# A two-layer attention, delta-rule and expert trunk on one core: four modulation slabs of the first layer loaded by the Activation queue and multiplied between convolution columns

## The chip, the core and the metric

The kernel runs on one core of a Trainium2 chip. The core has TensorE (PE, matmuls and transposes), VectorE (DVE), ScalarE (ACT, also called Activation), GpSimd (POOL) and SyncE (SP, which only issues transfers here). Sixteen DMA engines move data between HBM and the on-chip memory. ACT and POOL can issue transfers too, each on a queue of its own. The metric is the device time of one execution in microseconds, given as the median of several runs.

## The reference, cut to what matters

Two layers work on 128 context tokens and 256 latent tokens of width 1024, in float32.

```python
def modulation(cvec, lw):
    m = jax.nn.silu(cvec) @ lw["ada_w"] + lw["ada_b"]          # ada_w: (1024, 6144)
    return jnp.split(m[..., None, :], 6, axis=-1)               # sh1, sc1, g1, sh2, sc2, g2

def latent_layer(x, c, k_ctx, v_ctx, s_ctx, lw):                # context_layer: the same with c_ctx
    sh1, sc1, g1, sh2, sc2, g2 = modulation(c, lw)
    h = modulate(rms_norm(x, lw["norm1_g"]), sh1, sc1)
    zq, zk, zv, zqkv, zg, zb, za = jnp.split(h @ lw["w_in"], SPLITS, axis=-1)
    q, k, v = na_heads(zq, zk, zv, lw)
    o_na = neighbourhood_attention(q, k, v, k_ctx, v_ctx, lw["na_rpb"])
    gq, gk, gv, gg, gbeta = gdn_inputs(zqkv, zb, za, lw, axial=True)   # conv of 5 taps, SiLU, L2 norm
    o_g, _ = gdn_bidirectional(gq, gk, gv, gg, gbeta, s_ctx)           # chunked delta rule
    o_mix = jnp.concatenate([o_na, gdn_output(o_g, zg, lw["gdn_norm_g"])], axis=-1)
    x = x + g1 * (o_mix @ lw["w_out"])
    return x + g2 * hier_moe(modulate(rms_norm(x, lw["norm2_g"]), sh2, sc2), lw)
```

For the first half of a layer only `sh1` and `sc1` of the modulation are needed. `g1` is wanted at the output projection, and the last three at the expert part.

## The kernel before, in words

**Slabs.** Weights come in slabs of 2 MB. A layer's `ada_w` is twelve slabs: slab `i` holds 256 of the 1024 rows and 2048 of the 6144 columns, so four slabs (`SHARE`) make one third of the modulation. `w_in` is seven slabs (`win`) and `w_out` two (`wout`). They are held in a ring of five slots. SP loads them in the order of `PRE[l]` (`pre_slabs`), each after the job that last read its slot (`slab_done`). For the first layer the list is ada 0 to 3, the seven win slabs in the order 6, 3, 4, 5, 0, 1, 2, then ada 4 to 11 of this layer and ada 0 to 3 of the next, and wout. The second layer has no next one and so eight ada slabs behind its win slabs. The win slabs lie in slots 4, 0, 1, 4, 3, 4, 3; slot 2 holds none. All slabs behind them alternate between slots 4 and 3 (`LATE_SLOTS`).

**What else the ring holds.** From the convolution on, slots 0, 1 and 2 are the work space of the delta rule: `inv` and `inv_t[0]` lie in slot 0, `gT` and `inv_t[1]` in slot 1, `decays`, `sub_v` and `half_y` in slot 2. `decays` is first written by ACT at convolution column 5.

**One slab's product.** `ada_product` on PE multiplies 16 times into bank 3, which no other job uses in these stages. After four slabs DVE copies the bank to `mrow` (`ada_row`), PE turns it into columns (`ada_cols`, 8 small matmuls into a bank that DVE empties), and DVE adds the bias (`ada_col`).

**Order of a layer.** (1) Norm and modulation of the three token tiles, with the gate projection (win 6) between them. (2) The convolution stage: twelve column groups `f` of w_in (win 3, 4, 5), each 16 matmuls of 128x384; behind each, transposes of an earlier group (`conv_cols`), sums of decays (`decay_sums`, f = 5 to 10), and at f = 4 `gate_sums`, which waits for the small weights (`weights_in`). ACT empties each group to `conv_in`, DVE convolves, ACT applies SiLU, PE transposes back, ACT empties again. (3) Heads: `head_cols`, `head_products` for three token tiles, whose banks DVE turns into `weighed` and `inv`; then token-major projections (win 0, 1, 2), while DVE solves small triangular blocks (`substitution`). SP and POOL move these blocks through HBM (`blocks_out`, `blocks_back`, `inv_t`). (4) The mixing stage: ten steps of attention (`scores`, `probs_cols`, `weigh`), with the delta rule's parts `rule(k)` and the ada products between them, at 22 numbered points. `mixing_plan` spreads the products: with twelve slabs, the first before the steps and the others at points 4, 5, 6, 8, 9, 11, 12, 14, 15, 16 and 18; with eight, the others at 5, 7, 9, 11, 13, 15 and 17. (5) `gate_rows(1)`, transposes of `g1`, then the output projection, router and token lists. (6) Experts, whose weights (1 MB pieces) SP loads into the ring and the arena as pieces are given back.

**Banks.** DVE's jobs rotate over three PSUM banks and ACT's over three others: PE may fill one when the job three before it has been emptied (`dve_bank`, `act_bank`).

The work around the change is in the order written out by hand in each engine's block; waits are semaphore counts.

Of the kernel before, what the change touches and what calls it, by code (L numbers as in the profile page):

```python
# [14 lines left out]
P = 128  # L15
# [6 lines left out]
DEPTH = 2  # L22
# [10 lines left out]
SLAB = 4096  # L33
N_ADA, N_WIN, N_OUT = 12, 7, 2
EARLY = 4
PRE_SLOTS = 5
WIN_ORDER = [6, 3, 4, 5, 0, 1, 2]
WIN_SLOTS = [4, 0, 1, 4, 3, 4, 3]
# [20 lines left out]
N_STEPS = len(STEPS)  # L59
POINTS = 2 * N_STEPS + 2  # L60
RULE_AT = 3
SHARE = 4
BLOCK = 32
BLOCKS = P // BLOCK
MATS = TILES * GH
# [46 lines left out]
def pre_slabs():  # L112

    out = []
    for l in range(DEPTH):
        ada = [("ada", l, i) for i in range(EARLY, N_ADA)]
        if l + 1 < DEPTH:
            ada += [("ada", l + 1, i) for i in range(EARLY)]  # L120
        first = [("ada", 0, i) for i in range(EARLY)] if l == 0 else []
        out.append(first + [("win", l, j) for j in WIN_ORDER] + ada + [("wout", l, j) for j in range(N_OUT)])
    return out


def mixing_plan(slabs):
# [135 lines left out]
def program(nc, x_prompt, x_sample, c, cache_k, cache_v, state_ssm, c_ctx, ada_w, ada_b, norm1_g,  # L262
# [10 lines left out]
    with ctx:  # L273
# [236 lines left out]
        def place_of(slabs, i):  # L510

            first_win = [name[0] for name in slabs].index("win")
            if i < first_win:
                return i
            i -= first_win
            return WIN_SLOTS[i] if i < N_WIN else LATE_SLOTS[(i - N_WIN) % 2]
# [3 lines left out]
            earlier = [name for name in slabs[:i] if pre_slot[name] == pre_slot[slabs[i]]]  # L520
            return earlier[-1] if earlier else None

        for slabs in PRE:
            for i, name in enumerate(slabs):
                pre_slot[name] = place_of(slabs, i)
                held[pre_slot[name]] += 1
                pre_turn[name] = held[pre_slot[name]]

        def arrived(eng, *name):
            eng.wait_ge(slab_in[pre_slot[name]], 16 * pre_turn[name])  # L530
# [23 lines left out]
        def _(pe):  # L554
# [72 lines left out]
                ada_product(("ada", 0, i))  # L627
            ada_cols(("ada", 0, EARLY - 1), b_mods)
            for l in range(DEPTH):
                mixing = [name for name in PRE[l][EARLY if l == 0 else 0:] if name[0] == "ada"]  # L630
                plan = mixing_plan(mixing)

                def point(p):
# [74 lines left out]
                def ba_sums():  # L708

                    pe.wait_ge(dve_emptied, job["ba_part", l])  # L710
                    b = dve_bank("ba", l)
                    for t in range(TILES):
                        last = mm(b[:, t * BA:(t + 1) * BA], ba_part[:, t * P:(t + 1) * P], tab("pick_ba"))
                    last.then_inc(for_dve, 1)
# [31 lines left out]
                for f in range(12):  # L746
                    slab = ("win", l, 3 + f // 4)
                    if f % 4 == 0:
                        arrived(pe, *slab)
                    if f == 4:  # L750
                        gate_sums()
                    w = wide(pre_slot[slab])
                    b = act_bank("conv", l, f)
                    for k in range(KC):
                        last = mm(b[:, 0:TOK], w[:, k, (f % 4) * P:(f % 4 + 1) * P], hT[:, k, :], k == 0, k == KC - 1)
                    last.then_inc(for_act, 1)
                    slab_job[slab] = ("act", jobs["act"])
                    if f == 0:
                        ba_sums()
                    if 5 <= f < 11:  # L760
                        decay_sums(f - 5)
                    if f >= 2:
                        conv_cols(f - 2)
# [10 lines left out]
                def head_products(t):  # L774

                    pe.wait_ge(act_emptied, job["gT", l, t, 0])
                    for pair in range(2):
# [3 lines left out]
                            last = mm(b[:, 256 * i:256 * i + 256], gT[:, t, h, 0, :], flat(gT[:, t, h]))  # L781
                        last.then_inc(for_dve, 1)

                arrived(pe, "win", l, 0)
                head_cols(0)
                token_major(0, 0)
# [2 lines left out]
                head_cols(2)  # L789
                head_products(1)  # L790
                head_products(2)
                token_major(0, 1)
                token_major(0, 2)
                conv_cols(10)
# [484 lines left out]
        def _(sp):  # L1279
# [51 lines left out]
            for l in range(DEPTH):  # L1331
# [39 lines left out]
                        src = src[:, :, j * 512:(j + 1) * 512]  # L1371
                    sp.dma_start(dst, src).then_inc(slab_in[pre_slot[name]] if done is None else done, 16)

                first_mixing = [i for i, name in enumerate(PRE[l]) if name[0] == "ada" and i >= N_WIN][0]
                for i, name in enumerate(PRE[l]):
                    if i == first_mixing + 1:
                        blocks_back()
# [105 lines left out]
        def _(act):  # L1483
# [51 lines left out]
            for l in range(DEPTH):  # L1535
# [17 lines left out]
                modulated(l, 1, 2)  # L1553
                gate_tile(1)
                gate_tile(2)

                def token_tile(which, t):
                    b = filled("win", l, which, t)
# [43 lines left out]
                for c in range(12):  # L1602
# [2 lines left out]
                        act.wait_ge(conv_ready, 12 * l + c - 1)  # L1605
                    f(conv_in[:, c % 2, 2:2 + CTX], b[:, 0:CTX])
                    f(conv_in[:, c % 2, CTX + 6:CTX + 6 + LAT], b[:, CTX:TOK]).then_inc(act_emptied, 1)
                    if 5 <= c < 11:
                        decay_exp(c - 5)
                    if c >= 2:  # L1610
# [14 lines left out]
                def head_cols(t):  # L1625
                    for s in (1, 0):
                        b = filled("gT", l, t, s)
                        f(gT[:, t, :, 1 - s, :], b[:].rearrange("p (h n) -> p h n", h=GH)).then_inc(act_emptied, 1)

                head_cols(0)  # L1630
                act.wait_ge(act_emptied, job["conv_back", l, 9])
                token_tile(0, 0)
# [172 lines left out]
        def _(dve):  # L1805
# [119 lines left out]
            ada_col(("ada", 0, EARLY - 1))  # L1925
            for l in range(DEPTH):
                mod = mods[:, l]
                plan = mixing_plan([name for name in PRE[l][EARLY if l == 0 else 0:] if name[0] == "ada"])

                def point(p):  # L1930

# [184 lines left out]
                dve.wait_ge(gexp_ready, l + 1)  # L2116
                if l == 0:
                    dve.wait_ge(weights_in, 16 * N_SMALL)
                head_products(0)
                head_products(1)  # L2120
                vec.memset(sub_v[32:64], 0.0)
                head_products(2)
                convolve(10)
                convolve(11)
                qk_sums(0, 0)
# [443 lines left out]
        def _(pool):  # L2569
# [7 lines left out]
            for l in range(DEPTH):  # L2577
# [17 lines left out]
                mask_bias(0)  # L2595

                pool.wait_ge(for_act, job["conv", l, 7])
                for d in range(2):
                    gp.memset(inv_t[d], 0.0).then_inc(zeroed, 1)
                pool.wait_ge(raw_ready, 3 * (l + 1))  # L2600
# [132 lines left out]
```

## Time and profile before

| what | value |
|---|---|
| median of 3 runs | 1226.54 us (1225.91 to 1232.42) |
| profiled execution, its own time | 1225.16 us |
| its span in the profile | 1223.1 us |
| PE busy | 1104.9 us, 90% of the span |
| DVE, ACT, POOL busy | 555.9, 291.9, 110.1 us |
| DMA | 333.30 MB, mean 273 GB/s |
| mean granted clock of PE | 0.961 |

The profile is one execution. Its times are counted from the start of the span. "Idle before, releaser" names what ended an engine's idle time. A granted clock of 1.00 is 2.4 GHz, and 0.50 is 1.2 GHz. PEq, SPq and ACTq are sequencers: issues of transfers stand there. L577 is the helper for all matmuls and L580 that for all transposes, so tiles and shapes tell the jobs apart: an ada product is `bank<-ring,silu_w` x16, convolution columns are `bank<-hT,ring` 128x384 x16, `ada_cols` is `bank<-const,mrow` x8, the gate rows are `bank<-const,mod`.

### The profile page before, as it was taken

Reading aid. Unit: us, or ns where it says so; the run is one execution under the profiler, and the core shown is the slowest. Engines: PE = TensorE matmul, PEld = TensorE weight load, DVE = VectorE, ACT = ScalarE, POOL = GpSimd, SP = SyncE. Lnnn points to the kernel's source line nnn. Section 1 sums busy time; section 2 is a strip of 40 time slices with the busy share of each in tenths; the row PEclk is TensorE's granted clock in tenths of the full one; section 3 lists DMA queues with packets and bytes.
Section 4 is the critical chain, followed back from the end, with each engine's and each line's share of the span. In section 5 each row is a group of like instructions: output and inputs, shape, how many; then the busy total and the mean of one; then the engine's idle time right before and its main releaser. Section 6 shows DMA issues by size and latency. Waiting matters only on the chain.

```text
span 1223.1 us, 18762 instructions
## 1 busy us (share of the span) xinstructions
PE 1104.9 (90%) x7521; PEld 548.7 (45%) x7521; DVE 555.9 (45%) x1416; ACT 291.9 (24%) x717; POOL 110.1 (9%) x126
## 2 busy tenths in 40 slices
PE   4899999898999999978789999989999999997776
PEld 1455544475556333322245655446745733332222
DVE  1257896466447311210162678945744742111124
ACT  0347512323122110000021672232331310100000
POOL 0020023310001000000011000242000100000001
PEclk9899999799997999999989999988999799999998
DMA  8670134967935999999983203376495399999996
GB/s 356 204 196 1 70 95 130 288 259 282 407 155 215 416 424 425 424 426 424 421 335 109 72 1 95 138 164 235 183 379 200 145 418 421 425 424 425 425 424 264
DMA packets 90794, 333.30 MB, mean 273 GB/s; under 512 B 29631, under 2 KB 32071, under 8 KB 59975
## 3 DMA queue, kind: packets, MB, share of 16 engines
q1 hardware_dynamic: 80999, 299.66, 62.7%
q0 software_dynamic: 7392, 23.93, 5.8%
q10 hardware_dynamic: 2304, 8.39, 1.7%
q8 instruction: 63, 1.03, 0.3%
q14 instruction: 36, 0.29, 0.1%
HBM read 314.38 MB, written 17.56 MB: 271 GB/s over the span
## 4 chain that ended last, share of the span: by engine, by line
PE 71%; SPq 11%; DMA 9%; DVE 5%; issue 2%; ACT 2%; DVEq 0%; ACTq 0%
PE bank L577 66%; SPq L1318 10%; PE bank L580 5%; DMA arena<-in_moe_w_dram 4%; DMA ring<-in_ada_w_dram 3%; DMA ring<-in_w_in_dram 2%; ACT arena L1497 2%; DVE x L1831 1%; DVE ring L1831 1%; DVE x L1823 1%; DVE arena L1823 1%; DVE small L2144 0%; DVE small L1831 0%; DVE bank L1823 0%; SPq L1407 0%
## 5 line engine op out<-in xcount | busy, mean ns | idle before, releaser
L577 PE MATMUL bank<-ring,arena 128*32 128x512 f32 (+1 forms) x2272 | 328.6, 583 | 26.4 <-issue 12.5
L577 PE MATMUL bank<-arena 128*32 128x512 f32 (+3 forms) x1600 | 267.3, 562 | 18.7 <-DMA arena<-in_moe_w_dram 10.3
L1497 ACT ACTIVATE arena<-bank 128x512 f32<-128x512 f32 (+3 forms) x292 | 124.3, 467 | 577.0 <-PE bank L580 392.5
L577 PE MATMUL bank<-ring,hT 128*128 128x512 f32 x576 | 256.9, 600 | 3.7 <-DMA ring<-in_w_in_dram 2.7
L577 PEld LDWEIGHTS bank<-ring,arena 128*32 128x32 f32 (+1 forms) x2272 | 99.0, 114 | 214.4 <-issue 212.0
L577 PEld LDWEIGHTS bank<-ring,hT 128*128 128x128 f32 x576 | 108.5, 193 | 129.5 <-issue 126.3
L577 PE MATMUL bank<-hT,ring 128*128 128x384 f32 x384 | 128.3, 488 | 0.1
L1823 DVE TENSOR_TENSOR arena<-bank,mrow 128x512 f32<-128x512 f32 x36 | 24.9, 692 | 225.2 <-PE bank L577 225.2
L577 PEld LDWEIGHTS bank<-arena 128*32 128x32 f32 (+2 forms) x1600 | 80.6, 122 | 95.1 <-issue 78.3
L577 PEld LDWEIGHTS bank<-hT,ring 128*128 128x128 f32 x384 | 71.2, 190 | 46.9 <-issue 1.3
L580 PE MATMUL bank<-const,arena 128*128 128x128 f32 x443 | 66.7, 287 | 18.2 <-DMA x<-in_x_prompt_dram 8.5
L580 PEld LDWEIGHTS bank<-const,arena 128*128 128x128 f32 x443 | 52.2, 145 | 63.1 <-issue 57.1
L1823 DVE TENSOR_TENSOR hT<-hT,bank 128x512 f32<-128x512 f32 x18 | 19.3, 1074 | 133.0 <-PE bank L577 133.0
L1831 DVE SCALAR_TENSOR_TENSOR arena<-arena,cols 128x388 f32<-128x388 f32 x96 | 62.5, 651 | 3.4
L577 PE MATMUL bank<-ring 32*32 32x32 f32 (+3 forms) x976 | 58.6, 248 | 4.1 <-DVE ring L1831 2.3
L577 PE MATMUL bank<-ring,silu_w 128*32 128x512 f32 x384 | 48.6, 627 | 10.9 <-DMA ring<-in_ada_w_dram 10.9
L577 PEld LDWEIGHTS bank<-ring 32*32 32x32 f32 (+2 forms) x976 | 51.4, 156 | 14.8 <-issue 9.8
L1823 DVE TENSOR_TENSOR ring<-ring 112x30 f32<-112x30 f32 (+14 forms) x120 | 50.4, 420 | 4.1
L1497 ACT ACT_TABLE_LOAD x38 | 48.8, 1283 | 13.2 <-DVE cols L1836 10.0
L1497 ACT ACTIVATE hT<-bank 128x512 f32<-128x512 f32 (+1 forms) x32 | 18.9, 591 | 131.7 <-PE bank L577 94.6
L1497 ACT ACTIVATE arena<-bank,small 128x128 f32<-128x128 f32 (+2 forms) x74 | 34.9, 508 | 36.4 <-DVE small L2144 33.8
L2668 POOL DMA_INDIRECT arena<-tok_dram,idx x16 | 15.4, 962 | 242.5 <-issue 106.8
(162 smaller groups left out, 866.4 us busy)
## 6 DMA issues: line engine op xcount, KB each, us to landing
ring<-in_moe_w_dram SPq DMA_DIRECT2D x120, 1024.0 KB, 18.8
arena<-in_moe_w_dram SPq DMA_DIRECT2D x72, 1024.0 KB, 18.1
ring<-in_ada_w_dram SPq DMA_DIRECT2D x24, 2048.0 KB, 8.6
ring<-in_w_in_dram SPq DMA_DIRECT2D x14, 2048.0 KB, 9.7
ring<-in_w_out_dram SPq DMA_DIRECT2D x4, 2048.0 KB, 8.9
expert_dram<-arena ACTq DMA_DIRECT2D x16, 512.0 KB, 8.3
tok_dram<-arena POOLq DMA_DIRECT2D x6, 512.0 KB, 2.9
arena<-in_na_rpb_dram SPq DMA_DIRECT2D x16, 96.0 KB, 7.2
```

Of the source, the lines that this page charges most:

```text
L577: return nc.tensor.matmul(out, lhsT, rhs, start=start, stop=stop)
L580: return nc.tensor.transpose(out, src, ident[0:rows_, 0:rows_])
L1318: sp.dma_start(dst.rearrange("p (o k n) -> p o k n", o=1, k=src.shape[2]), src).then_inc(done, 16)
L1497: return nc.scalar.activation(out, in_, func, **kw)
L1823: return vec.tensor_tensor(out, a, b, op)
L1831: return vec.scalar_tensor_tensor(out, a, s, b, op0, op1)
L2668: pool.indirect_dma_start(out=x_e[:, c_ % 2, :], out_offset=None, in_=tok_dram, in_offset=bass.IndirectOffsetOnAxis(ap=idx[:, column(c_):c ...
```

## The change

In the first layer ada slabs 4 to 7 leave SP's list. ACT issues their loads, into slots 2, 0, 0 and 1 (`MIDDLE_SLOTS`): the first after the third gate tile, the second when convolution group 4 has been emptied (slot 0's win slab was last read by group 3), the third and fourth at group 8. PE multiplies the first two behind groups 2 and 6, the other two behind the loop over the groups, and makes the columns after the head products. ACT waits for the first product before it writes `decays`, and for the fourth before it writes `gT`; POOL waits for the fourth before it clears `inv_t`; DVE copies the row ahead of its head products. The mixing stage of the first layer is left with eight slabs and `mixing_plan` places them. The second layer is as before.

```diff
+MIDDLE_LAYERS = 1
+MIDDLE_SLOTS = [2, 0, 0, 1]
...
+def middle_slabs(l):
+    return [("ada", l, EARLY + i) for i in range(SHARE)] if l < MIDDLE_LAYERS else []
+
+def mixing_slabs(l):
+    here = [("ada", l, i) for i in range(EARLY, N_ADA)] + [("ada", l + 1, i) for i in range(EARLY) if l + 1 < DEPTH]
+    return [name for name in here if name not in middle_slabs(l)]
...
 # tensor
-                mixing = [name for name in PRE[l][EARLY if l == 0 else 0:] if name[0] == "ada"]
+                mixing, middle = mixing_slabs(l), middle_slabs(l)
...
                     if f == 0:
                         ba_sums()
+                    if middle and f in (2, 6):
+                        ada_product(middle[f // 4])
                     if 5 <= f < 11:
                         decay_sums(f - 5)
...
+                for slab in middle[2:]:
+                    ada_product(slab)
                 arrived(pe, "win", l, 0)
                 head_cols(0)
...
                 head_products(1)
                 head_products(2)
+                if middle:
+                    ada_cols(middle[-1])
                 token_major(0, 1)
...
 # scalar
                 gate_tile(2)
+                middle = middle_slabs(l)
+                def load_middle(i):
+                    src = ada_w[l].rearrange("(k p) n -> p k n", p=P)[:, 2 * i:2 * i + 2, 2048:4096]
+                    s = pre_slot[middle[i]]
+                    act.dma_start(slot(s).rearrange("p (k n) -> p k n", k=2), src).then_inc(slab_in[s], 16)
+                if middle:
+                    if l == 0:
+                        act.wait_ge(ada_full, EARLY)
...
+                    load_middle(0)
...
+                    if middle and c == 4:
+                        act.wait_ge(for_act, job["conv", l, 3])
+                        load_middle(1)
+                    if middle and c == 8:
+                        act.wait_ge(ada_full, slab_job[middle[1]][1])
+                        load_middle(2)
+                        act.wait_ge(for_act, job["conv", l, 7])
+                        load_middle(3)
+                    if middle and c == 5:
+                        act.wait_ge(ada_full, slab_job[middle[0]][1])
                     if 5 <= c < 11:
                         decay_exp(c - 5)
...
+                if middle:
+                    act.wait_ge(ada_full, slab_job[middle[3]][1])
                 head_cols(0)
...
 # vector
+                if middle:
+                    ada_row(middle[-1])
                 head_products(0)
                 head_products(1)
                 vec.memset(sub_v[32:64], 0.0)
                 head_products(2)
+                if middle:
+                    ada_col(middle[-1])
                 convolve(10)
...
 # gpsimd
                 pool.wait_ge(for_act, job["conv", l, 7])
+                if middle_slabs(l):
+                    pool.wait_ge(ada_full, slab_job[middle_slabs(l)[3]][1])
                 for d in range(2):
                     gp.memset(inv_t[d], 0.0).then_inc(zeroed, 1)
```

## Rows read from the trace of the kernel before

**Rows 1.** Page, 40 slices of the span, what the DMA engines moved.
```profile
GB/s 356 204 196 1 70 95 130 288 259 282 407 155 215 416 424 425 424 426 424 421 335 109 72 1 95 138 164 235 183 379 200 145 418 421 425 424 425 425 424 264
```

**Rows 2.** Chain that ended last, 60 to 360 us, by line.
```profile
by line: PE bank L577 80.0%; DMA ring<-in_ada_w_dram 10.7%; PE bank L580 4.0%; ACT arena L1497 1.9%; DVE ring L1831 1.1%; SPq L1359 0.9%; issue 0.7%; DVE arena L1823 0.6%; SPq L1372 0.1%; ACT hT L1497 0.1%; ACTq L1488 0.0%; DVEq L2079 0.0%;
```

**Rows 3.** Windows: busy us of PE, PEld, DVE, ACT, POOL; clock; DMA share; GB/s.
```profile
60.00:80.00 20.00, 20.00 (x77) 11.03 (x76) 7.06 (x15) 6.11 (x11) 0.00 (x0) 1.00 0.65 164
...
100.00:120.00 20.00, 19.97 (x67) 11.53 (x66) 11.97 (x21) 16.90 (x44) 1.41 (x2) 1.00 0.00 1
...
214.00:222.00 8.00, 4.77 (x41) 2.48 (x40) 2.32 (x5) 2.77 (x12) 6.85 (x10) 0.91 0.93 187
222.00:232.00 10.00, 8.73 (x199) 5.42 (x200) 4.28 (x11) 3.58 (x9) 1.18 (x1) 0.50 1.08 265
...
841.00:851.00 10.00, 9.47 (x122) 6.68 (x119) 7.66 (x19) 2.95 (x9) 0.00 (x0) 1.00 0.73 281
```

**Rows 4.** Waits of PE, 200 to 312 us: total, times, longest.
```profile
PE bank L577 <- DMA ring<-in_ada_w_dram: 7.0, 3, 3.0
```

**Rows 5.** Timeline of PE, layer 0, mixing stage and after: start, duration.
```profile
214.26 1.92 PE L577 MATMUL bank<-ring,silu_w 128*32 128x512 f32 x16
...
252.04 0.96 PE L577 MATMUL bank<-const,mrow 128*128 128x8 f32 x8
252.92 1.93 PE L577 MATMUL bank<-ring,silu_w 128*32 128x512 f32 x16
254.78 0.88 PE L577 MATMUL bank<-arena 128*64 128x128 f32 x12
...
310.93 1.97 PE L580 MATMUL bank<-const,mod 128*128 128x128 f32 x16
...
386.70 0.37 PE L577 MATMUL bank<-tokid_b,arena 128*128 128x2 bf16 x9
```

**Rows 6.** The same of layer 1.
```profile
811.08 1.92 PE L577 MATMUL bank<-ring,silu_w 128*32 128x512 f32 x16
...
833.99 2.80 PE L577 MATMUL bank<-ring,silu_w 128*32 128x512 f32 x16
...
898.20 1.99 PE L580 MATMUL bank<-const,mod 128*128 128x128 f32 x16 [0.28 <-DVE mod L1823]
...
973.99 0.37 PE L577 MATMUL bank<-tokid_b,arena 128*128 128x2 bf16 x9
```

**Rows 7.** Timeline of PE and DVE, convolution stage and heads of layer 0.
```profile
69.53 10.57 PE L577 MATMUL bank<-hT,ring 128*128 128x384 f32 x32
...
85.76 0.96 PE L577 MATMUL bank<-small,const 128*128 128x12 f32 x8
...
104.08 1.02 PE L577 MATMUL bank<-arena,const 128*128 128x512 f32 x2
...
152.36 1.12 DVE L1831 SCALAR_TENSOR_TENSOR ring<-bank,small,ring 128x128 f32<-128x128 f32 x4
152.80 13.90 PE L577 MATMUL bank<-ring,hT 128*128 128x512 f32 x32
```

**Rows 8.** Timeline of ACT, POOL and ACT's queue: start, duration.
```profile
62.38 0.60 ACT L1497 ACTIVATE arena<-bank 128x512 f32<-128x512 f32 x1 [6.27 <-PE bank L577]
...
82.63 4.66 POOL L2574 TENSOR_TENSOR arena<-arena,gdn_g 128x512 f32<-128x512 f32 x3 [74.75 <-DMA w_rt<-in_moe_w_re_dram]
...
92.44 0.72 ACT L1497 ACTIVATE arena<-bank 128x128 f32<-128x128 f32 x3 [4.17 <-PE bank L577]
...
441.53 0.36 ACTq L1776 DMA_DIRECT2D expert_dram<-arena  x1
```

**Rows 9.** Page, DMA issues: count, KB each, median us to landing.
```profile
ring<-in_ada_w_dram SPq DMA_DIRECT2D x24, 2048.0 KB, 8.6
...
expert_dram<-arena ACTq DMA_DIRECT2D x16, 512.0 KB, 8.3
...
x<-in_x_sample_dram SPq DMA_DIRECT2D x1, 1024.0 KB, 24.3
```

More of the change, by code:

```diff
@@ L35 @@
 EARLY = 4
+SHARE = 4
+MIDDLE_LAYERS = 1
+MIDDLE_SLOTS = [2, 0, 0, 1]
 PRE_SLOTS = 5
@@ L61 @@
 RULE_AT = 3
-SHARE = 4
 BLOCK = 32
@@ L117, in pre_slabs @@
     for l in range(DEPTH):
-        ada = [("ada", l, i) for i in range(EARLY, N_ADA)]
-        if l + 1 < DEPTH:
-            ada += [("ada", l + 1, i) for i in range(EARLY)]
         first = [("ada", 0, i) for i in range(EARLY)] if l == 0 else []
-        out.append(first + [("win", l, j) for j in WIN_ORDER] + ada + [("wout", l, j) for j in range(N_OUT)])
+        out.append(first + [("win", l, j) for j in WIN_ORDER] + mixing_slabs(l) + [("wout", l, j) for j in range(N_OUT)])
     return out
+def middle_slabs(l):
[3 more added lines that the diff above has]
+    return [name for name in here if name not in middle_slabs(l)]
 def mixing_plan(slabs):
@@ L521, in held_before @@
             return earlier[-1] if earlier else None
[L523 to L527, printed above, removed]
+        for l, slabs in enumerate(PRE):
+            fore = slabs.index(("win", l, WIN_ORDER[-1])) + 1
+            places = [(name, place_of(slabs, i)) for i, name in enumerate(slabs)]
+            for name, s in places[:fore] + list(zip(middle_slabs(l), MIDDLE_SLOTS)) + places[fore:]:
+                pre_slot[name] = s
+                held[s] += 1
+                pre_turn[name] = held[s]
         def arrived(eng, *name):
@@ L1372, in load_slab @@
                     sp.dma_start(dst, src).then_inc(slab_in[pre_slot[name]] if done is None else done, 16)
-                first_mixing = [i for i, name in enumerate(PRE[l]) if name[0] == "ada" and i >= N_WIN][0]
+                first_mixing = PRE[l].index(mixing_slabs(l)[0])
                 for i, name in enumerate(PRE[l]):
@@ L1555, in _ @@
                 gate_tile(2)
+                middle = middle_slabs(l)
[6 more added lines that the diff above has]
+                        act.wait_ge(ada_full, EARLY)
+                    else:
+                        act.wait_ge(es["y_full"], 3 * BATCHES * l)
+                    load_middle(0)
                 def token_tile(which, t):
@@ L1927, in _ @@
                 mod = mods[:, l]
-                plan = mixing_plan([name for name in PRE[l][EARLY if l == 0 else 0:] if name[0] == "ada"])
+                middle = middle_slabs(l)
+                plan = mixing_plan(mixing_slabs(l))
                 def point(p):
```

## The prediction

> **What bounds the kernel now.** I read the page's slices first; at full load the DMA engines move 424 to 425 GB/s, and there are two stretches where they move almost nothing, the convolution stages of the two layers [rows 1]. Then the chain of waits, cut to 60 to 360 us, the region that the diff touches: 80% of it is TensorE (PE) itself, and 10.7% is `ring<-in_ada_w_dram`, the loads of modulation slabs [rows 2]. The windows say where the room is: from 100 to 120 us PE is busy 19.97 of 20 us at a granted clock of 1.00, and the DMA share is 0.00; ScalarE (ACT) is busy 16.9 there [rows 3]. Then PE's own waits in the mixing stage: 7.0 us in three waits for such slabs [rows 4]. So layer 0's mixing stage, which I measure from its first product (214.26) to the gate rows (310.93), is 96.67 us long [rows 5] and passes twelve slabs through two ring slots. Layer 1's mixing stage has only eight slabs and is otherwise the same code: from 811.08 to 898.20, 87.12 us [rows 6]. The new plan of layer 0 has eight slabs too, at the points that the same formula gives, so layer 1 is the nearest row for it.
>
> What follows the gate rows takes the same time in both layers: to the first list of tokens it is 75.77 us in layer 0 and 75.79 in layer 1 (386.70 and 973.99 [rows 5, 6]). So a shift of layer 0's gate rows should reach the end of the span whole.
>
> **The change, part by part.**
>
> *Products moved forward.* A slab's product is 16 matmuls; at full clock the next instruction starts 1.86 us after it (252.92 to 254.78 [rows 5]). In the convolution stage PE has no hole to put it in [rows 3], so four of them cost 4 x 1.86 = 7.44 us there.
>
> *Their columns.* `ada_cols` costs 0.88 us (252.04 to 252.92 [rows 5]). It takes a bank from the rotation of three that VectorE (DVE) empties, right after `head_products(2)`, and so must wait until DVE is through with the job three before, the second pair of tile 1. DVE ends that at 152.36 + 1.12 = 153.48, while PE is free at 152.80 now and goes on with token columns that need an ACT bank [rows 7]. That is a new wait of 0.68 us. It stays when all is later, because DVE's work on the pairs starts with PE's first pair. DVE's own additions are a row copy, ahead of the first pair, for which DVE waits for PE anyway, and a column add of 0.2 us on a chain that moves later by less than PE does. Sum of the front: 7.44 + 0.88 + 0.68 = 9.0 us.
>
> *The loads and the waits that they bring.* An issue on ACT's queue costs ACT 0.36 us [rows 8]; four make 1.4 us, in a stage where ACT has 3.1 of 20 us free [rows 3], and each product gives it 1.86 us more. I take nothing. The first slab is issued once ACT has emptied the third gate tile, 62.38 + 0.60 = 62.98 [rows 8], and is wanted when convolution columns 2 are done, 69.53 + 10.57 = 80.1 [rows 7]: 17.1 us later. Ada loads landed after 8.6 us in the median [rows 9]. But this one shares the engines with a projection slab and the bias rows: a share of 0.65 from 60 to 80 us, 13.0 us of full work [rows 3]; 2.1 MB at 424 GB/s [rows 1] add 5.0, and 62.7 + 18.0 = 80.7 is the latest by plain addition. Early bound 71.6 and no wait, late bound a wait of 0.6 us; I take 0, since the late bound needs this slab to be served last of all. What SP has queued there counts too: its small weights let GpSimd (POOL) start at 82.63 [rows 8], and PE asks for them in `gate_sums` at 85.76 [rows 7]. Pushed back by the whole 5.0 us they come at 87.6, and PE then asks at 85.76 + 1.86 = 87.6: no cost, and no margin. The Trainium skill (DMA: Bandwidth & Descriptors, section "Issuing engines are not separate DMA queues") says that transfers of SP, ACT and POOL run on the same 16 engines and interleave, and that another issuer saves only issue time. By that rule a second queue wins no bandwidth: the 5.0 us come on top, as I have added them, and the sum stays. Stores of 512 KB on ACT's queue, the size of a quarter slab, landed after 8.3 us beside SP's expert loads [rows 9], which agrees.
>
> The second slab is issued after columns 4 are emptied, 92.44 + 0.55 now [rows 8] and 94.85 then, and wanted at the end of columns 6, 104.08 + 1.86 = 105.9 [rows 7]: 11.1 us against 8.6. The third and fourth go out two columns of 6.35 us and two products after that, near 121.5, and are wanted from 140; 8.6 + 5.0 us fit into that, with idle engines [rows 3]. ACT's new waits are for products that PE did before the bank which ACT has just emptied; behind them stand decay exponentials, squares and the banks that PE asks for next, none late unless a slab is. POOL's clearing of `inv_t` now waits for the fourth product, near 144; its results are wanted after 200 us. SP's own order only gets shorter. All of this at 0.
>
> *What the mixing stage gives back.* Taken out are four products, one column step and the slab waits: 7.44 + 0.88 + 7.0 = 15.3 us if nothing takes their place. But the products also filled PE's waits in the softmax chain (scores, DVE's maxima, ACT's exponentials, transposes). So the bounds are -15.3, by removal, and -9.55, by layer 1 (87.12 against 96.67). I take -9.55: it is the same eight-slab code, measured.
>
> *Sum.* 9.0 - 9.55 = -0.55 us. The profiled execution took 1225.16 us, 2.06 more than its span and 1.38 less than the median of the three runs. So 1224.6 for such an execution, and 1226.0 beside the median of 1226.54. A change under 0.5% (6.1 us) can hardly be told from none for this kernel.
>
> **Rivals.**
>
> *The removal counts in full.* If no wait takes the place of the old ones, the sum is 9.0 - 15.3 = -6.3 and the time 1220.2 us. For it: layer 0 has DMA waits in its mixing stage and layer 1 the same chain without them, so the two need not be alike in the rest. Against it: 15.3 minus 9.55, 5.8 us, is what layer 1 shows as not given back, and I know of nothing in its code that layer 0 lacks.
>
> *The first slab comes late* (the case on the other side). Its product stands in PE's order behind columns 2, so from 17.1 us after its issue each microsecond late is one of the total. A load behind a full queue took 24.3 us here (`x<-in_x_sample_dram` [rows 9]); that would be 7.2 us of wait, 1233.2 us, slower. For it: two queues at full load beside each other have not been seen in this stage. Against: the engines have 7 us of room in these 20, and the 24.3 us were behind 8 MB.
>
> *The clock falls more often.* PE was busy 4.77 of 8 us, and then the granted clock is 0.50, its level of 1.2 GHz, from 222 to 232 us [rows 3]. In layer 1 a product as late as 833.99 still takes 2.80 us in place of 1.93 [rows 5, 6]. With fewer fillers, light steps could fall to that level again; one stretch of 10 us costs about 5, so 1231. Layer 1 is back at 1.00 in the window from 841 on [rows 3] with the same plan, which speaks against it. The Trainium skill (TensorE: Matmul & The Clock Gate, section "HAM oscillation — how this bites in real kernels") says that waits between bursts of matmuls let the clock go back to half; the trace agrees at these two places.
>
> *It does not remove the slab waits.* Two slots remain, and each slab still waits for the product before the last. Then 9.0 - 8.3 = +0.7, 1227.2. Layer 1 shows that eight slabs in two slots pass in 87 us, so this is unlikely.
>
> **How the numbers follow.** Forecast, with leftovers from -4 to +3 us around 1226.0: 0.74. Removal in full, 1220.2: 0.08. First slab late, 1233: 0.08. Clock, 1231: 0.06. Slab waits stay, 1227: 0.04. The full removal straddles the bound of 6.1 us and the late slab lies just above it: faster 0.06, same 0.85, slower 0.09. The range reaches down to near the full removal, 1221.0, and up to 1230.5, past half of the late-slab wait.
>
> **What would show it.** Right: four products of 1.9 us more between 80 and 150 us, the head products 7.4 us later, a wait of some 0.7 us ahead of new `mrow` columns there, the first mixing product at 223.3 and the gate rows at 310.4, with 87 us between them and no PE wait for `in_ada_w_dram`; all later stages moved by the same half microsecond. Wrong: a PE wait for a slab at columns 2 or 6, a wait in `gate_sums`, a granted clock under 1.00 before 200 us, or a mixing stage under 84 or over 90 us. What would upset the number most is a layer 0 that is not like layer 1.

## The result: 0.6% faster, and outside the range

The changed kernel takes 1220.34 us in the median of 20 runs (1213.79 to 1226.76), the kernel before beside it 1226.64 us (20 runs, 1218.43 to 1233.84). The ratio is 0.9941, 95% interval 0.9923 to 0.9959: 7.2 us less, 5.0 to 9.4. The forecast was 1226.0 and the range ended at 1221.0. The profiled execution of the changed kernel is one of its long ones, 1226.13 us, with a span of 1223.9 us at a mean granted clock of 0.962. So its length as a whole says nothing, and its stages have to be read one by one: over the whole span PE's gaps by "issue" (idle time that ends with no semaphore) add up to 34.0 us in it and to 26.9 us in a second profile of the same kernel, 25.1 and 33.7 us in two profiles of the kernel before.

"The front" is from here on all that stands ahead of the first product of the mixing stage. Changed kernel, waits of PE for DVE from 60 to 210 us (in total, times, longest; 0.4 us for ACT stand beside them, as in the kernel before):

```profile
PE bank L589 <- DVE ring L1875: 1.6, 3, 0.7
```

What the DMA engines moved in the 40 slices, and the issues of modulation slabs on ACT's queue (count, KB each, median us to landing; SP's twenty had 8.7 us):

```profile
GB/s 357 203 234 103 202 95 99 216 225 242 378 104 318 420 424 424 424 426 424 418 211 136 46 39 97 114 193 202 199 400 147 215 415 425 424 425 424 425 422 195
...
ring<-in_ada_w_dram ACTq DMA_DIRECT2D x4, 2048.0 KB, 9.4
```

The empty fourth slice of the kernel before [rows 1] now carries 103 GB/s. Timeline of PE, front (start, duration):

```profile
80.02 1.92 PE L589 MATMUL bank<-ring,silu_w 128*32 128x512 f32 x16
...
106.16 1.92 PE L589 MATMUL bank<-ring,silu_w 128*32 128x512 f32 x16
...
140.28 3.64 PE L589 MATMUL bank<-ring,silu_w 128*32 128x512 f32 x32
...
160.82 1.03 PE L589 MATMUL bank<-const,mrow 128*128 128x8 f32 x8 [0.65 <-DVE ring L1875]
```

The four products stand at 80, 106 and 140 us, and the columns behind a wait of 0.65 us. Nothing waits for a slab. The two marks of the mixing stage of layer 0 answer to [rows 5]:

```profile
223.25 1.92 PE L589 MATMUL bank<-ring,silu_w 128*32 128x512 f32 x16
...
304.83 1.39 PE L592 MATMUL bank<-const,mod 128*128 128x128 f32 x11
```

The front is 223.25 - 214.26 = 8.99 us longer. The mixing stage is 304.83 - 223.25 = 81.58 us in place of 96.67. The stage behind the gate rows, up to the first list of tokens at 377.44, is 72.61 us in place of 75.77. Waits of PE in the mixing stage, the changed kernel and then the kernel before (there beside the 7.0 us for slabs [rows 4]):

```profile
PE bank L589 <- ACT arena L1515: 4.1, 10, 0.7
PE bank L592 <- DVE arena L1867: 2.3, 1, 2.3
PE bank L592 <- DVE arena L1871: 2.1, 2, 1.2
PE bank L589 <- DVE ring L1875: 0.3, 1, 0.3
```

```profile
PE bank L580 <- DVE arena L1823: 2.9, 1, 2.9
PE bank L577 <- ACT arena L1497: 2.9, 7, 0.5
PE bank L580 <- DVE arena L1827: 1.0, 1, 1.0
```

The slab waits are gone. The waits for ACT and DVE grow from 6.8 to 8.8 us. Removal in full, less these 2.0 us, is 15.3 - 2.0 = 13.3 us.

Windows over whole stages: the kernel before (mixing stage of layer 0, of layer 1, stage behind the gate rows), then the changed one (the same three):

```profile
214.26:310.93 96.67, 82.58 (x957) 53.46 (x957) 52.79 (x138) 29.69 (x98) 13.04 (x15) 0.93 0.81 282
811.08:898.20 87.12, 76.37 (x885) 52.13 (x885) 51.95 (x137) 29.85 (x98) 13.33 (x15) 0.90 0.68 226
310.93:386.70 75.77, 72.84 (x325) 49.14 (x324) 40.31 (x151) 17.91 (x42) 1.62 (x3) 0.91 0.59 234
```

```profile
223.25:304.83 81.58, 72.82 (x885) 50.08 (x885) 51.00 (x136) 29.59 (x98) 11.54 (x12) 0.96 0.71 237
807.63:894.97 87.34, 76.86 (x885) 52.08 (x884) 51.86 (x137) 29.86 (x98) 13.17 (x15) 0.90 0.68 225
304.83:377.44 72.61, 68.85 (x324) 44.85 (x324) 40.24 (x151) 17.69 (x42) 1.62 (x3) 0.98 0.57 229
```

These six rows hold a part of the answer. In one execution of the changed kernel the two mixing stages, both with eight slabs and both with 885 matmuls, last 81.58 and 87.34 us. The column to look at is the granted clock: 0.96 against 0.90. A mean of 0.90 over 87.12 us is (1 - 0.90) x 2 x 87.12 = 17.4 us at 0.50 (17.1 by the records of the clock); 0.96 over 81.58 us is 6.5 (6.8). The stage that I used as the measure, layer 1 of the kernel before, was such a slow one, with a gap of 1.64 us by "issue" besides. Layer 0 of the kernel before, with which I compared it, had 13.7 us at 0.50 and no such gap. So the clock alone parts those two by little; what it is worth is worked out below.

### The profile page after: what moved, and what is told of

The parts are those of the page before. It is cut to its first block, busy times and chain, and to the rows that moved or that the text cites. A ratio compares the mean times of both kernels' runs of the same rounds, so it can differ in the third digit from the quotient of the medians.

```text
span 1223.9 us, 18765 instructions
## 1 busy us (share of the span) xinstructions
PE 1103.7 (90%) x7521; PEld 540.6 (44%) x7521; DVE 554.1 (45%) x1416; ACT 291.9 (24%) x717; POOL 109.7 (9%) x126
## 4 chain that ended last, share of the span: by engine, by line
PE 71%; SPq 10%; DMA 7%; DVE 6%; issue 4%; ACT 2%; ACTq 0%; DVEq 0%
PE bank L589 67%; SPq L1336 9%; PE bank L592 4%; DMA ring<-in_w_in_dram 2%; ACT arena L1515 2%; DMA ring<-in_moe_w_dram 2%; DMA arena<-in_moe_w_dram 2%; DVE small L2193 1%; DVE x L1875 1%; DVE ring L1875 1%; DVE arena L1867 1%; DVE x L1867 1%; DVE bank L1867 1%; DVE small L1875 0%; SPq L1425 0%
## 5 line engine op out<-in xcount | busy, mean ns | idle before, releaser
L589 PE MATMUL bank<-ring,arena 128*32 128x512 f32 (+1 forms) x2272 | 337.8, 594 | 33.6 <-issue 21.5
L589 PE MATMUL bank<-arena 128*32 128x512 f32 (+3 forms) x1600 | 272.6, 564 | 19.2 <-DMA arena<-in_moe_w_dram 9.8
L589 PEld LDWEIGHTS bank<-arena 128*32 128x32 f32 (+2 forms) x1600 | 81.1, 123 | 89.5 <-issue 72.4
L1875 DVE SCALAR_TENSOR_TENSOR arena<-arena,cols 128x388 f32<-128x388 f32 x96 | 65.1, 678 | 3.4
L589 PEld LDWEIGHTS bank<-ring 32*32 32x32 f32 (+2 forms) x976 | 51.1, 154 | 14.7 <-issue 8.5
L1515 ACT ACTIVATE arena<-x 128x512 f32<-128x512 f32 (+1 forms) x18 | 13.9, 771 | 96.9 <-DVE x L1867 68.9
## 6 DMA issues: line engine op xcount, KB each, us to landing
ring<-in_w_in_dram SPq DMA_DIRECT2D x14, 2048.0 KB, 10.2
```

Of the source, the lines that this page charges most:

```text
L589: return nc.tensor.matmul(out, lhsT, rhs, start=start, stop=stop)
L1515: return nc.scalar.activation(out, in_, func, **kw)
L1875: return vec.scalar_tensor_tensor(out, a, s, b, op0, op1)
```

## The experiments

All were timed in five rounds, beside the kernel before on the same chip. Ratios are to that kernel.

**The two kernels again.** No edit: the changed kernel, and the kernel before.

> The changed kernel once more, unchanged, for a second profile and more times. Theory A (removal in full): the first layer's mixing stage, first product to gate rows, is 81.6 us again within 1 us, whatever the clock does elsewhere, and the ratio is 0.993 to 0.996. Theory B (clock): the stage's length follows the time that TensorE spends at 0.50 in it: 78.2 us plus half of the low time, so 81.6 with 6.8 us low and about 85 with 13.7; the ratio then depends on how often each kernel meets the low clock.

> The kernel before against itself: how far two equal kernels part in this measurement, and a second profile. Both theories: ratio 1.000 within 0.002. Theory A: mixing stage of the first layer 96.7 within 1 us. Theory B: 89.8 us plus half of the low time in it, and a span that changes by some 0.4 us for each microsecond of low clock.

Measured: 1220.39 us, ratio 0.9950 (0.9929 to 0.9971), and 1224.15 us, 0.9996 (0.9976 to 1.0015). The gain repeats. The profiles give other stages, though: the mixing stage of layer 0 is 98.77 us in the kernel before and 81.48 in the changed one, and that of layer 1 is 85.77 and 85.57. The same code spreads by microseconds from one execution to the next. Neither theory holds for both kernels: theory A has its 81.6 us and misses the 96.7, theory B has 98.3 us for the kernel before (89.8 and half of 17.1), which fits, and 79.9 for the changed one (78.2 and half of 3.4), which does not.

**The modulation slabs 4 to 7 left out.** From the changed kernel, without their loads, products, row, column step and waits. In their place `mods` of the gate and the second shift are copied from the first shift.

```diff
-                    if middle and f in (2, 6):
-                        ada_product(middle[f // 4])
...
-                for slab in middle[2:]:
-                    ada_product(slab)
...
-                    ada_row(middle[-1])
+                    vec.tensor_copy(mods[:, 0, 16:24, :], mods[:, 0, 0:8, :])
+                    vec.tensor_copy(mods[:, 0, 24:32, :], mods[:, 0, 0:8, :])
```

> The changed kernel without its four middle slabs at all: no loads, products, row or columns for them; DVE copies the first layer's shift over the gate and second shift, so 8 MB are not read and the output is another. The mixing stage keeps its eight slabs. Tells the price of the front alone. If the front costs 9.0 us and reaches the end whole, this is 9.0 faster than the changed kernel, near 1211 beside 1226.6, a ratio of 0.987. Rival: the front is partly hidden by something that ends last anyway, then only 3 to 5 us under the changed kernel, 0.990 to 0.992. Mixing stage as in the changed kernel, 79 to 87 us by its clock.

Measured: 4291.71 us, ratio 3.50. With these values the path for crowded experts ran (the profile reads 937 MB from HBM in place of 314), so this time says nothing on the question. The next version takes the negative of the first shift as the second:

```diff
-                    vec.tensor_copy(mods[:, 0, 24:32, :], mods[:, 0, 0:8, :])
+                    ts(mods[:, 0, 24:32, :], mods[:, 0, 0:8, :], -1.0)
```

> As the run that left the four slabs out, but with a stand-in for their modulation that keeps the experts' token counts under their limits (gate from the first shift, second shift from its negative), so that the path for crowded experts is not taken. No loads, products, row or columns for the four slabs. Front price of 9.0 us whole: the first mixing product at 214.3 to 215, the mixing stage 81 to 87 us, and 9 us under the changed kernel, near 1211, ratio 0.987 to 0.988. Rival (front hidden in part): 0.990 to 0.992.

Measured: 1217.19 us, ratio 0.9923 (0.9899 to 0.9948). Its first mixing product starts at 214.12 us, so all of the front's 9 us is gone in the profile, but its mixing stage had 17.1 us of low clock and took 86.53. By time it is 0.22%, 2.7 us, under the changed kernel (0.9923 against 0.9945, the mean of the latter's two ratios), with intervals of 0.2 to 0.25% on each side. So the expected 9.0 us did not come by time. Its six runs spent 96 us at the lower clock in the mean (from each run's span and mean clock), and the kernel before beside them 84. At 0.30 us each (worked out below) that is 3.7 us, so the run is too blunt to price the front.

**Three loads left out of the kernel before.** The slabs that PE waited for; their products read what lies in the slots.

```diff
+        SKIPPED = [("ada", 0, 6), ("ada", 1, 2), ("ada", 1, 3)]
...
-                held[pre_slot[name]] += 1
+                held[pre_slot[name]] += 0 if name in SKIPPED else 1
...
+                    if name in SKIPPED:
+                        continue
```

> The kernel before without the loads of the three slabs for which TensorE waited in the first layer's mixing stage (its third, eleventh and twelfth); their products stay and read what lies in the slot, so the modulation is another. Tells the waits from the products. If the slab waits are the only thing that a load costs there, the mixing stage is 7.0 us shorter, 89.7, and the ratio 0.994 to 0.995. Rival: the softmax chain takes half of it back, 93 us and 0.997. A clock effect would show as a stage off by half of the difference in low time.

Measured: 1218.84 us, ratio 0.9948 (0.9928 to 0.9968), 6.4 us less. The mixing stage is 89.94 us, with 1.3 us of slab wait left and 6.8 us of low clock. The ratio is the one expected if a load costs its wait and nothing else. With the products kept, the slab waits alone are worth what they lasted (7.0 - 1.3 = 5.7 us, and 92.9 - 87.9 = 5.0 us once the lower clock and the gaps are taken off as in the table below). This already speaks against the prediction's term, which left 9.55 us for waits, four products and a column step together.

**The first mixing product behind the first `weigh`,** in both layers of the changed kernel.

```diff
-                ada_product(mixing[0])
...
                     weigh(step)
+                    if step == 0:
+                        ada_product(mixing[0])
```

> The changed kernel with the first product of the mixing stage behind the first weigh, in both layers, so that it fills TensorE's wait for DVE's scaled scores (2.3 us in the first layer, 3.0 in the second). If the chain of the softmax only needs to start earlier, probs_cols(0) and (1) come 1.86 us earlier in each layer: 3.7 us off, and more if the low clock starts later or not at all, up to 8. Rival: the next waits (1.2 us at probs_cols(2)) grow by what this one loses, and nothing changes.

Measured: 1218.74 us, ratio 0.9939 (0.9916 to 0.9961). The interval holds the changed kernel's ratio, so the gain of some 1 us is not shown. The wait in layer 0 fell from 2.26 to 1.32 us.

**The same change in both layers.**

```diff
-MIDDLE_LAYERS = 1
+MIDDLE_LAYERS = 2
```

> The changed kernel with the same four slabs moved in the second layer too (its mixing stage keeps four). There TensorE waits for no slab now, so nothing but the place of the products changes. If products only move: front +9.0, mixing -8.3, so +0.7 and more where the softmax chain takes its waits back; I expect +3, ratio to the kernel before 0.997. If moving them also shortens the stretch at low clock as it did in the first layer: -3, ratio 0.992.

Measured: 1221.71 us, ratio 0.9951 (0.9931 to 0.9971). Where no slab wait is to be removed, moving four products buys nothing: layer 1 from its first products with `x` (628.77 us, in the changed kernel 625.54) to the mixing stage takes 190.97 us in place of 182.09, so 8.9 more, and the mixing stage 77.93, or 72.4 with its 10.2 us of low clock and its gap of 2.4 taken off, so 7.6 less than 80.0. That is close to the bare move of the products (+0.7 us expected), and neither the +3 nor the -3 is shown.

**The keys scaled early:** POOL's `keys_at_end(0)` ahead of `bias_rows(pool, l, 1)`, both layers.

```diff
-                bias_rows(pool, l, 1)
                 keys_at_end(0)
+                bias_rows(pool, l, 1)
```

> The changed kernel with POOL's first scaling of keys ahead of its eight bias transfers in both layers, so that it no longer runs beside DVE's scaling of scores in the second layer (two passes of 256 columns there took 1.36 to 1.66 us in place of 0.76). If that overlap is what makes the second layer's wait 3.0 us instead of 2.25, the wait falls to 2.3 and the passes to 0.76; the first layer does not change. Time: 0.7 us off, or 2 to 4 if the stretch at low clock (10 to 14 us in the second layer, 3 to 7 in the first) hangs on the length of that wait.

Measured: 1222.27 us, ratio 0.9949 (0.9925 to 0.9974). The wait of 3.0 us in layer 1 fell to 2.3 and DVE's two passes ahead of it from 1.49 to 0.76, as expected, and that moved no time that can be seen. What its profile shows besides is the clearest case of the second disturbance beside the clock, the gaps by "issue". Timeline of PE, layer 0:

```profile
238.49 0.65 PE L589 MATMUL bank<-ring 32*32 32x32 f32 x53
243.76 0.84 PE L589 MATMUL bank<-ring 32*32 32x32 f32 x43 [4.62 <-issue]
```

and what the DMA queues did from 241 to 242.5 us (packets, MB, share of 16 engines):

```profile
q8 instruction: 1, 0.02, 4.3%
```

PE stops for 4.62 us in the midst of 96 equal matmuls, with no semaphore to wait for. From 234 to 241 us the instruction queue moved nothing; at 241.13 us one block of 16 KB starts on it, lands after 1.03 us, and 1.6 us later PE goes on. All 23 such gaps in the mixing stages of the thirteen profiles (all but that of the run with crowded experts) end the same way, 1.3 to 1.6 us after a block of this queue has landed. That the block held PE's instructions is inferred from this timing. The Trainium skill (Trainium Architecture — The Big Picture, section "Inside one NeuronCore") has each engine run a stream of instructions of its own. That this stream came late here, in mid-kernel, is what the timing suggests; no run changed it.

**Fillers.** Dummy matmuls of 128x512 while PE would wait for the softmax chain: eight per mixing stage in the kernel before, seven in the changed one. Their output is not read. Each of these calls stands as two matmuls in the trace.

```diff
+                def filler(n_):
+                    if jobs["dve"] >= 3:
+                        pe.wait_ge(dve_emptied, jobs["dve"] - 2)
+                    for _ in range(n_):
+                        mm(bank[jobs["dve"] % 3][:], ident, const[:, 0:512])
...
+                    filler({1: 5, 2: 2}.get(step, 0))
                     probs_cols(step)
```

> The kernel before with eight dummy matmuls of 128x512 added per mixing stage (six ahead of the probability transposes of step 1, two ahead of those of step 2), whose output nobody reads: they keep TensorE at work while it would wait for the softmax chain. Theory A (the eight slabs taken out are worth about 13.2 us of mixing stage at an undisturbed clock): with less low clock in the stage it is 92 to 94 us in layer 0 with its three slab waits left. Rival B (my prediction's proxy, 9.55): the stage stays near 96. In time about 1224 to 1226, or 2 to 4 below if the fillers spare low clock.

> The changed kernel with seven such dummy matmuls per mixing stage (five and two). Theory A: 79 to 81 us in layer 0 and the same in layer 1, so 13 us under the twelve-slab stage of the run beside it, and as a whole 4.2 us shorter than that run's kernel (9.0 paid in front, 13.2 given back). Rival B: 87 us in both layers, and the two kernels within 1 us of one another.

Measured: 1233.61 us, ratio 1.0046 (1.0022 to 1.0069), and 1224.92 us, 0.9985 (0.9958 to 1.0013). The mixing stages of layer 0 are 97.78 and 86.94 us, that of layer 1 in the second kernel is 88.60. These lengths miss theory A's (92 to 94 and 79 to 81) and look like rival B's (96 and 87), but they hold the fillers' own cost. The six ahead of step 1 in the kernel before:

```profile
219.26 5.42 PE L577 MATMUL bank<-const 128*128 128x512 f32 x12
```

That is 0.90 us for each filler, 5.42 + 1.98 = 7.4 us for the eight, and they took the place of 3.9 us of waits for DVE. So a stage gets 3.5 us longer, which is what its length says once the lower clock and the gaps are taken off (96.4 us against 92.9). The difference of the two kernels is 10.84 us in the profiles, with no microsecond at 0.50 in the longer stage and 6.8 of them in the shorter. At 0.30 us each (worked out below), and with "issue" gaps of 1.4 and 1.9 us taken off, it is 97.78 - 1.4 - (86.94 - 1.9 - 2.0) = 13.3, of which up to 0.9 is the one filler more. By the ratios it is 7.5 us net of the front (3 to 12 with both intervals), up to 1.8 of it the two fillers more, where theory A had 4.2 and rival B under 1. The fillers lean to theory A and do not decide by themselves.

They did spare low clock: the twelve runs of each kernel spent some 72 and 67 us at the lower clock in the mean, those of the kernel before beside them 90. But they cost more than that gives back.

**The front alone.** The changed kernel's work in the convolution stage, and all twelve slabs in the mixing stage as before.

```diff
-    return [("ada", l, EARLY + i) for i in range(SHARE)] if l < MIDDLE_LAYERS else []
+    return [("mid", l, EARLY + i) for i in range(SHARE)] if l < MIDDLE_LAYERS else []
...
-    return [name for name in here if name not in middle_slabs(l)]
+    return here
```

> The front's price alone: the changed kernel's four loads on the Activation queue, its four products, row, column step and waits in the convolution stage are there, and the mixing stage keeps all twelve slabs as before (the four slabs are multiplied twice). Theory A: first mixing product at 223.3 us (+9.0), mixing stage 93 to 97 us, time +9.0, so 1235 and a ratio of 1.0073. Rival: the front costs only 3 to 5 us in time, as the run with the middle slabs left out suggested by its time (3.2 us under the changed kernel); then 1230.

Measured: 1233.51 us, ratio 1.0047 (1.0024 to 1.0069), so +5.8 us, 2.9 to 8.5. Window of its mixing stage, and PE's slab waits in it:

```profile
223.99:319.15 95.16, 83.36 (x958) 52.94 (x957) 52.32 (x138) 29.64 (x98) 11.57 (x12) 0.93 0.79 279
```

```profile
PE bank L589 <- DMA ring<-in_ada_w_dram: 4.5, 2, 2.8
```

The expected ratio of 1.0073 lies just above the interval, and the rival's 1230 us (1.003) lie in it. The stage starts at 223.99, 9.7 us later than in the kernel before and 8.8 later than in its repetition (215.24). It is also shorter than with the old front: the slab waits are 4.5 us where three profiles of the old front had 7.0, 6.8 and 7.2. 9.0 - 2.5 = 6.5 fits the measured 5.8. But this is one profile, and why a longer front should shorten these waits I have not found: the second slab is issued 0.1 us behind the first product with either front. The clock is another candidate: these twelve runs spent 82 us at the lower clock in the mean and the kernel before beside them 90, which at 0.30 us each hides 2.6 us of the front's price. No run parts the two.

This run also prices the other half by time. From this kernel to the changed one only the four slabs leave the mixing stage, and the ratio goes from 1.0047 to 0.9945: 0.0102 x 1226.3 = 12.5 us less. With the intervals of these ratios that is 9 to 16 us, so by time alone 9.55 is not excluded.

**Two of the edits together:** first product behind the first `weigh`, and keys early.

> The changed kernel with the first mixing product moved behind the first step's weighing and the scaling of the keys on GpSimd ahead of the bias rows, in both layers. The two edits alone gave 1218.7 and 1222.3 beside 1220.4. If the first is worth 1 us and the second shortens one wait of 3.0 us per layer to 2.3: 1218 to 1219.5. Rival: nothing beyond the changed kernel, 1220.4, since what is left of the waits is the softmax chain itself.

Measured: 1217.30 us (1212.26 to 1222.25), ratio 0.9926 (0.9900 to 0.9953). It is the lowest of all kernels that compute the whole, 2.3 us under the changed kernel by the ratios, but the intervals overlap, so it beats the kernel before for certain and the changed one only probably. The expected 1218 to 1219.5 and the rival's 1220.4 both lie inside its interval.

## Why the prediction was wrong

**The front (+9.0): right.** 8.99 us in the profile, with the wait of 0.68 us ahead of the columns measured as 0.65. The loads brought no wait. The first slab landed after 11.0 us, between my bounds (the late one should have been 62.98 + 18.0 = 81.0, not 80.7). For the small weights I was right by a margin that I had not seen. `gate_sums` starts at 87.75 us, and POOL, which waits for the same weights, starts at 88.08, so they were there later than my 87.6. But the first eight matmuls of `gate_sums` do not read them; the wait stands ahead of the next ones, at 88.64 us.

**The mixing stage (-9.55): the step that failed.** The mechanism (products, a column step and slab waits out, some waits back) was right; the size was read from one stage of one profile. I took 87.12 us of layer 1 against 96.67 of layer 0 and wrote that it is "the same eight-slab code, measured". What I did not look at was how long each of the two was at the lower clock, the gap of 1.64 us by "issue" in the former, and how far the same stage spreads from one execution to the next. Thirteen eight-slab mixing stages stand in the profiles of the kernels without fillers and with the first product in its old place (both layers of the changed kernel, of its repetition, of the one with the slabs left out and of the one with the keys early; layer 0 of the two-layer kernel; layer 1 of the kernel before, of its repetition, of the one with three loads less and of the one with the front alone). They last from 81.48 to 88.09 us. Take off each stage's "issue" gaps, and a straight line through the rest is 80.0 us plus 0.30 for each microsecond at 0.50. What it leaves is 0.4 us (root mean square). Some of them:

| stage | length | at 0.50 | issue gaps | length less 0.30 x low, less gaps |
|---|---|---|---|---|
| before, layer 1 (the proxy) | 87.12 | 17.1 | 1.6 | 80.4 |
| changed, layer 0 | 81.58 | 6.8 | 0 | 79.5 |
| changed, layer 1 | 87.34 | 17.1 | 1.5 | 80.7 |
| changed again, layer 0 | 81.48 | 3.4 | 0.4 | 80.1 |
| keys early, layer 0 | 88.09 | 13.7 | 4.6 | 79.4 |
| before, layer 0, twelve slabs | 96.67 | 13.7 | 0 | 92.6 |
| before again, layer 0, twelve slabs | 98.77 | 17.1 | 0.5 | 93.2 |

So the kernel's own difference between twelve slabs and eight is 92.9 - 80.0 = 12.9 us by the profiles, 13.3 by the waits, and 12.5 (9 to 16) by time. In the profiles it is not 9.55. Layer 0 alone says the same: with the moved front it is 79.3 to 80.1 us in four profiles, 13.3 below the 92.9. With 13 the sum would have been 9.0 - 13 = -4.0 and the forecast 1222.5, inside the range that was given and 2.2 us above the result. My reading that 5.8 us of the removal are given back was 2.0 us of waits, 1.6 us of the proxy's gap, 1.0 us of its clock (0.30 x 3.4), and 1.2 us that I cannot place.

**What is left.** Measured are 7.2 us (5.0 to 9.4) and, in the repetition, 0.0050 x 1225.0 = 6.1 us (3.6 to 8.7). The 4.0 us lie inside the second interval and outside the first. So the term that was mis-sized makes up some 3.5 of the 6 us by which the forecast was off, and the rest is open. The two prices by time do not close it: 12.5 and 5.8 us are both counted from the run with the front alone, so their difference, 6.7, is the measured gain once more. Nor does the clock of the repetition: the changed kernel was at the lower clock for 84 us in the mean there and the kernel before for 85. A front that costs less than its instructions would close it. The slab waits of the run with the front alone point that way, and its clock points the other.

**What follows the gate rows moves by the same amount: wrong as a measure, open as a rule.** The two equal lengths that I saw, 75.77 and 75.79, were both at 13.7 us of low clock. The same stage took 71.5 us in five other profiles (3.4 us of low clock in each). Two equal numbers from one execution looked like a constant and were not.

**The rivals.** The removal in full (1220.2 us, given 0.08) gave the number, in part by luck: the profiles show 13 of its 15.3 us, and what they do not explain makes up for the rest. Its mechanism is nearer to the runs than mine. What I held against it, the 5.8 us that [rows 6] seemed to keep, was for the most part not a property of the code. The late slab did not come. The clock did not fall more often: the changed kernel's layer 0 stage had 6.8 us at the lower clock, the one before 13.7, and over the profiles without fillers stages with twelve slabs have 6.8 to 17.1 and stages with eight 3.4 to 20.5. The slab waits did not stay.

## What to carry to other kernels

A stage that serves as the measure for another must first be cleared of what only its execution had: read the granted clock over just that stretch, and the gaps by "issue", for both, or take the same stage from several profiles. Where a proxy (9.55) and a count of what is removed (15.3) lie far apart, name the instructions that fill the difference; if none can be named, distrust the proxy, as here the count was the nearer of the two. A transfer wait on the engine that sets the end was worth its whole length here (5.7 us of waits, 6.4 us of time). To move its product into a full stage cost the product, and once a column step and a wait of 0.65 us. Without a wait to remove, the same move (both layers) gained nothing.

## What the runs showed of the hardware

- **The lower clock comes at different places in each execution of one kernel.** The changed kernel was at 0.50 for 92.1 us of one execution (span 1223.9) and for 59.5 us of another (1210.7). In the mixing stage it comes with PE's waits. The first long stretch at 0.50 of layer 0 in the kernel before starts at 220.5 us, within PE's wait of 2.88 us for DVE. Where fillers took the place of these waits, one of four stages had no low clock, and in the other three it set in within 1 us of the end of a gap by "issue" of 1.3 to 4.2 us. The Trainium skill (TensorE: Matmul & The Clock Gate, section "HAM oscillation — how this bites in real kernels") puts it on waits between bursts, and here the trace agrees. It is less clear behind the gate rows: from 372 to 384 us of the kernel before the clock is 0.50 throughout, while PE is busy 10.84 of 12 us with transposes and small products. PE waited 1.00 and 0.77 us before it fell at 370.7 and once, for 1.16 us, during it.
- **PE seems to run out of instructions** in a row of small matmuls, by the timing told above. The gaps are 1.2 to 4.2 us in layer 1's mixing stage in each of thirteen profiles, and 0.2 to 4.6 us in nine of the thirteen in layer 0's.
- **DVE and POOL in each other's way.** Two DVE passes over 128x256 from SBUF take 1.38 us while POOL works on its keys (kernel before, at 220.10 us; POOL from 218.80 for 2.06 us), and 0.76 us in the changed kernel, where POOL is through before:

```profile
220.10 1.38 DVE L1823 TENSOR_TENSOR arena<-arena,small 128x256 f32<-128x256 f32 x2
```

```profile
229.09 0.76 DVE L1867 TENSOR_TENSOR arena<-arena,small 128x256 f32<-128x256 f32 x2
```

  The Trainium skill (SBUF — State Buffer, section "Who interferes with whom") says that a DVE instruction with two SBUF inputs contends with a POOL instruction that reads SBUF. By this rule the later of the two waits; the trace agrees, with 0.6 us, and PE's wait behind it is 2.9 against 2.3 us. The run with the keys early shows the cause: with POOL's work out of the way, layer 1's two passes fell from 1.49 to 0.76 us. In layer 0 the moved front does the same by itself: the wait is 2.25 or 2.26 us in all five profiles that have it with the old order of products and no fillers, and 2.8 to 3.05 us in the four of the old front.
- **A second queue slows the first.** SP issued eight bias rows in 14.93 us from 62.77 in the changed kernel, while the slab came by ACT's queue, and in 9.60 us in the kernel before. It is the load that does it: the eight profiles with a load on ACT's queue there have 14.7 to 15.6 us, the five without one 9.5 to 9.9, among them the changed kernel with its four slabs left out (9.76). The small weights queued behind them let POOL start at 88.08 us in place of 82.63 [rows 8], 5.45 us later, as long as one slab takes alone at full load (5.0 by my working).
